# Feed-forward of a two-layer model: seven block products per matrix in place of eight

## The reference, cut to what matters

```python
x = x + merged @ w_out[l]
h2 = rmsnorm_2(x, g_mlp[l])
x = x + jnp.square(jax.nn.relu(h2 @ w_ff1[l])) @ w_ff2[l]        # w_ff1 1024x4096, w_ff2 4096x1024
ple_gate = jax.nn.sigmoid(rmsnorm_2(x, g_ple[l]) @ w_ple_gate[l])
x = x + (p[l] @ w_ple[l]) * ple_gate
return rmsnorm_2(x, g_final)
```

## Time and profile before

| | |
|---|---|
| median of 3 runs | 3937.43 us (3936.14 to 3940.52) |
| the profiled execution: its own time | 3931.09 us |
| the profiled execution: its span | 3929.4 us |
| mean granted TensorE clock | 0.959 |
| TensorE busy in the span | 3606.5 us (92%) |
| `Tail`, first matmul to end | 3021.8 to 3929.4 us |
| DMA in the feed-forward | 97 GB/s |

### The profile page before, as it was taken

The page is one execution under the profiler, slowest core; times in us unless marked ns, Lnnn a source line. Parts: engine busy times, 40 slices in busy tenths (PEclk is TensorE's granted clock), DMA queues, the critical chain, the costliest instruction groups (busy, mean ns, idle before and its releaser), DMA issues. The chain is left out here.

```text
span 3929.4 us, 44017 instructions
## 1 busy us (share of the span) xinstructions
PE 3606.5 (92%) x16732; PEld 2857.8 (73%) x16732; DVE 2196.8 (56%) x2464; ACT 1568.7 (40%) x2086; POOL 1111.4 (28%) x569
## 2 busy tenths in 40 slices
PE   7899998586999999779899999999798999999997
PEld 3678887465787878557677577777676888888886
DVE  5579467646888888767553322222255643353338
ACT  4322234535777777635223222222322332232233
POOL 1232210334111111234312122222243444444443
PEclk9899999797999999889999999999899999999999
DMA  5312346657999999834311311111354223333333
GB/s 196 97 54 88 121 141 205 208 179 272 399 395 402 402 396 402 346 137 153 134 65 60 109 59 62 66 57 58 129 182 140 96 92 97 98 96 97 97 113 123
DMA packets 176113, 650.33 MB, mean 166 GB/s; under 512 B 21392, under 2 KB 56560, under 8 KB 159824
## 3 DMA queue, kind: packets, MB, share of 16 engines
q1 hardware_dynamic: 134464, 553.24, 39.1%
q10 hardware_dynamic: 31696, 65.07, 4.4%
q0 software_dynamic: 9792, 29.81, 2.0%
HBM read 540.71 MB, written 107.34 MB: 165 GB/s over the span
## 5 line engine op out<-in xcount | busy, mean ns | idle before, releaser
L3743 POOL TENSOR_TENSOR t_wl<-t_raw,t_wh 128x1024 fp32r<-128x1024 f32 x160 | 386.8, 2418 | 521.1 <-ACT t_wh L3789 521.1
L100 PE MATMUL m_b<-b_high,m_high 128*128 128x512 f32 x960 | 404.6, 421 | 8.9 <-POOL m_low L2616 7.0
L102 PE MATMUL m_b<-b_high,m_low 128*128 128x512 f32 x960 | 382.8, 399 | 0.0
L101 PE MATMUL m_b<-b_rest,m_high 128*128 128x512 f32 x960 | 382.3, 398 | 0.0
L2614 POOL TENSOR_TENSOR m_high<-m_raw,m_one 128x1024 fp32r<-128x1024 f32 x60 | 119.0, 1983 | 796.9 <-PE m_b L102 727.7
L100 PE MATMUL t_b<-b_high,t_wh 128*128 128x512 f32 x768 | 301.9, 393 | 15.2 <-POOL t_wl L3743 15.2
L101 PE MATMUL t_b<-b_rest,t_wh 128*128 128x512 f32 x768 | 299.6, 390 | 0.0
L102 PE MATMUL t_b<-b_high,t_wl 128*128 128x512 f32 x768 | 299.6, 390 | 0.0
L3789 ACT ACTIVATE t_wh<-t_raw 128x1024 fp32r<-128x1024 f32 x160 | 169.1, 1057 | 311.4 <-PE t_b L102 290.4
L100 PE MATMUL zs_z<-zs_hs,zs_high 128*128 128x512 f32 (+1 forms) x584 | 226.8, 388 | 8.5 <-DVE zs_hs L310 8.0
L3882 DVE TENSOR_TENSOR t_x<-t_x,t_b 128x512 f32<-128x512 f32 x80 | 55.0, 687 | 317.2 <-PE t_b L102 317.2
(11 more groups left out here) (658 smaller groups left out, 8672.5 us busy)
## 6 DMA issues: line engine op xcount, KB each, us to landing
moe_raw<-in_expert_w SPq DMA_DIRECT2D x79, 2048.0 KB, 10.1
ex_raw<-in_expert_w SPq DMA_DIRECT2D x39, 2048.0 KB, 10.7
t_raw<-in_w_ff SPq DMA_DIRECT2D x128, 512.0 KB, 3.4
m_raw<-in_w_ug SPq DMA_DIRECT2D x60, 512.0 KB, 4.4
yrows<-ex_y ACTq DMA_DIRECT2D x38, 512.0 KB, 11.1
gates<-m_ob SPq DMA_DIRECT2D x32, 512.0 KB, 2.9
me_g<-gates SPq DMA_DIRECT2D x32, 512.0 KB, 3.7
zs_raw<-in_w_in_s SPq DMA_DIRECT2D x29, 512.0 KB, 3.5
```

Of the source, the lines that this page charges most:

```text
L100: nc.tensor.matmul(out, w[0], x[0], start=first, stop=False)
L101: nc.tensor.matmul(out, w[0], x[1], start=False, stop=False)
L102: return nc.tensor.matmul(out, w[1], x[0], start=False, stop=last)
L3743: self.nc.gpsimd.tensor_tensor(self.wl[u % self.NW][:], self.raw[u % 2][:], self.wh[u % self.NW][:].bitcast(F32), ALU.subtract).then_inc(s ...
```

## The change

Both matrix products are done by Strassen's scheme on 2x2 blocks: seven products of half the depth in each direction where the plain scheme has eight.

**First matrix.** w_ff1 is cut by input half (512 of 1024) and output half (tile g against tile g + 16), the tokens in two halves. For each of 16 pairs g there are 7 products of 4 x 3 = 12 matmuls (112 in all). Four of them need a sum of weight blocks (`weight_sum`, VectorE, 128x512), and four need a combination of blocks of the normalised x (made once, in place of x, `t_made`; x itself is first written to DRAM, `spill`). The seven PSUM results are combined by VectorE (`c11`, `u2`, `c12`, `c22`, `c21`) into four hidden tiles, which get relu and square in one VectorE instruction (`bend`), and five combinations of them (`mix`, `mix21`); seven tiles of 256 KB a pair are written to DRAM (`keep`).

**Second matrix.** Seven passes over 16 of those tiles each; a pass has 4 output groups of 4 chains' parts, 12 matmuls a part (112 parts, v = 0 to 111), one bank per group of 4 parts. Each part's weights are loaded as one or two 256 KB blocks (2 KB rows) and, in five of the seven passes, summed by VectorE (`weight_sum2`). The hidden tiles come back from DRAM one by one (`hidden`), each split again (`hid_high` ScalarE, `hid_low` VectorE). A group's bank is added to or subtracted from one or two tiles of x (`update`, 48 additions in all).

**Around them.** Weight tiles of WO and GATE keep 24 matmuls but share four wh/wl buffers of 128x512, so two units deep in place of three; raw is four tiles deep; seven banks in place of six. GATE units all come after the feed-forward. The hand-written order of the starts (`load`, `scalar`, `vector`) is new.

The diff, cut to its core; after the DMA queue (`load`) come a stretch of ScalarE with `evict(f)`, then VectorE from the start of the first matrix:

```diff
-    NB, NW, NHID, NPW = 6, 3, KD + 1, 8
+    NB, PAIRS, FIRST = 7, 16, 14
+    RING = (1, 2, 5, 6, 3, 7, 4)
+    PASSES = (((1, 0), (1, 1), 1, ((1, 0, 1), (1, 1, -1))),
+              ((1, 1), None, 0, ((0, 0, 1), (1, 0, 1))),
+              ((0, 0), (1, 1), 1, ((0, 0, 1), (1, 1, 1))),
+              ((0, 1), (1, 1), -1, ((0, 0, 1),)),
+              ((0, 0), (0, 1), 1, ((0, 0, -1), (0, 1, 1))),
+              ((0, 0), None, 0, ((0, 1, 1), (1, 1, 1))),
+              ((1, 0), (0, 0), -1, ((1, 1, 1),)))
+    def products(self):
+        return [(g, x) for x in (1, 2, 3, 5, 6, 7, 4) for g in range(2)] + [(g, x) for g in range(2, self.PAIRS) for x in self.RING]
...
+        def weights(v):
+            (r, c), second, _, _ = self.PASSES[v // 16]
+            n, q = v % 16 // 4, v % 4
+            if v >= 4:
+                sp.wait_ge(self.split, self.NF + v - 3)
...
+                sp.dma_start(self.raw[:, v % 4, half(i)], self.A["w_ff2"][n + 4 * r][:, a:a + BANK]).then_inc(self.ff2_in[v % 4], 16)
...
+        for g in range(self.PAIRS - 2):
+            sp.wait_ge(self.split, self.at[g, 4] + 1)
+            pair(g + 2)
+            keep_b11(g)
+            keep(g)
...
+        for v in range(8, self.NV):
+            weights(v)
+            if v + 12 < self.NV:
+                hidden(v + 12)
...
+        for f in range(10, self.NF):
+            evict(f)
+            high(f + 4)
+            for p in {105: range(0, 4), 106: range(4, 8), 107: range(8, 12), 108: range(12, 15), 110: range(15, 16)}.get(f, ()):
+                hid_high(p)
...
+        mean(1)
+        for x in (5, 6):
+            weight_sum(1, x)
+        invert(1)
+        for k in range(4, KD):
+            scale(1, k)
+            if k > 4:
+                y_low(1, k - 1, KD + k - 5)
+        weight_sum(1, 3)
+        y_low(1, KD - 1, KD + 3)
+        for j in range(4):
+            scale(1, j)
+        for j in range(4):
+            dve.wait_ge(self.scaled, KD + 4 + j + 1)
+            V.tensor_tensor(self.X(j, 0), self.X(j, 1), self.X(j, 0), ALU.subtract).then_inc(self.t_made, 1)
+        weight_sum(1, 7)
+        for j in range(4):
+            V.tensor_tensor(self.X(j, 1), self.X(4 + j, 1), self.X(j, 1), ALU.subtract).then_inc(self.t_made, 1)
+        t_low(0)
...
+        for g in range(2):
+            bend11(g)
+            bend12(g)
+            bend22(g)
+            mix(g)
+        weigh(18)
+        for g in range(2):
+            c21(g)
+            mix21(g)
...
+        def step(f):
+            g, x = self.order[f]
+            if x == 2:
+                c11(g)
+                bend11(g)
+            if x == 6:
+                u2(g)
+            if x == 3:
+                c12(g)
+                bend12(g)
+            if x == 7:
+                c22(g)
+                bend22(g)
+                mix(g)
+            if x == 4:
+                c21(g)
+                mix21(g)
+            weigh(f + 5)
...
+               hid=(7, 16, P, BANK))
...
+    A["w_ff1"], A["w_ff2"] = tiles(J["w_ff1"][0]), tiles(J["w_ff2"][0])
```

More of the change, by code:

```diff
@@ L3645 @@
 class Tail:
[L3651 to L3652 removed]
+    NB, PAIRS, FIRST = 7, 16, 14
+    RING = (1, 2, 5, 6, 3, 7, 4)
+    PASSES = (((1, 0), (1, 1), 1, ((1, 0, 1), (1, 1, -1))),
[6 rows of a table added]
+    NF, NV = 112, 112
+    WO_UNITS = GATES = 2 * KD
     def __init__(self, nc, s, A, R, C, out, high, rest, gains):
         self.nc, self.A, self.R, self.C, self.out, self.h, self.gains = nc, A, R, C, out, (high, rest), gains
[L3656 to L3662, removed]
[L3663 to L3676 removed]
@@ L3678, in order @@
[L3678 to L3714, removed]
+        self.order = self.products()
@@ new lines, in __init__ @@
+        self.at = {u: f for f, u in enumerate(self.order)}
+        first = [(g, x) for g in range(2) for x in (5, 6, 3, 7)]
+        sums = first + [u for u in self.order if u[0] >= 2 and u[1] in (5, 6, 3, 7)]
+        self.sum_at = {u: i + 1 for i, u in enumerate(sums)}
+        self.wsum_at, self.loads = [], []
+        for v in range(self.NV):
+            two = self.PASSES[v // 16][1] is not None
+            self.wsum_at.append((self.wsum_at[-1] if v else 0) + two)
+            self.loads.append((self.loads[v - 4] if v >= 4 else 0) + (32 if two else 16))
@@ L3718, in load, with spill @@
         tiles_of = lambda r, c: r.rearrange("k p t -> p k t")[:, :, half(c)]
[L3719 to L3723, removed]
+        def spill(i):
+            c, n = divmod(i, KD)
+            sp.wait_ge(self.added, i + 1)
+            sp.dma_start(self.R["xb"][n][:, half(c)], self.X(n, c)).then_inc(self.spilled[c], 16)
@@ new lines, in load @@
+        keep(14)
+        for p in range(4, 12):
+            hidden(p)
+        for v in range(2, 4):
+            weights(v)
+        keep_b11(15)
+        weights(4)
+        for p in range(12, 15):
+            hidden(p)
+        weights(5)
+        hidden(15)
+        weights(6)
+        for p in range(16, 20):
+            hidden(p)
+        weights(7)
+        keep(15)
+        for c in range(2):
+            sp.wait_ge(self.kept_b11[c], 128)
+            sp.wait_ge(self.kept[c], 96 * 8)
@@ new lines, in scalar @@
+        for u in range(2):
+            wo_high(u)
+        for u in range(self.WO_UNITS):
+            c, n = divmod(u, KD)
+            act.wait_ge(self.wo_used, u + 1)
+            if u + 2 < self.WO_UNITS:
+                wo_high(u + 2)
+            else:
+                for f in range(2):
+                    high(2 * (u + 2 - self.WO_UNITS) + f)
+            if u == KD:
+                root(0)
+            act.wait_ge(self.added, u + 1)
+            square(c, n)
+            if KD + 1 <= u < KD + 5:
+                for k in range(2 * (u - KD - 1), 2 * (u - KD)):
+                    y_high(0, k, k)
```

638 lines of the change are left out of this document (512 added, 126 removed).

## The result

The changed kernel takes **3914.88 us** (median of 4 runs, 3910.47 to 3918.32) against 3936.78 us for the kernel before in the same comparison (3932.81 to 3940.52): a ratio of 0.9945 with a 95% interval from 0.9931 to 0.9959, so 21.9 us faster (16 to 27). The forecast was 3882, that is 55 us; the sign held, the size did not. One run of before (4320 us, granted clock 0.80) and one of e4 (14617 us, 0.23) were slow, and the ratios leave them out.

The account below looks back on a forecast made before the run. TensorE's own work was taken to bound the kernel (busy 92% of the span). Removing 87.0 and 7.2 us and giving back 26, 6, 3, 1 and 3 made -55: 3882 us from 3937.4, range 3850 to 3930.

Parts of the forecast that it names:

- Removed: Feed-forward: 384 fewer matmuls at 0.2267 us save 87.0 us; the old hand-over's stall of 7.2 us goes too.
- First matrix, steady: 0: Steady pairs of the first matrix: VectorE and GpSimd keep up with TensorE's 19.04 us, adding 0, bounds 0 to 45.
- rival B: First matrix: VectorE sets the pace, 1.5 to 3.2 us a pair, adding 21 to 45: 3903 to 3927; chance 0.21.
- Second matrix, steady, and its loads: 0: Second matrix: VectorE and GpSimd keep pace (0, bounds 0 and 10), and 256 KB loads at 261 GB/s add 0.
- rival C: Second matrix: loads don't keep up, below 222 GB/s; at 200 GB/s the time is 3975 us; chance 0.08.
- Start of the first matrix: +26: First matrix's start: TensorE waits 19 us in early products and 7 more at product 19; bounds 12 and 40.
- Hand-over: +6, bounds 0 and 14: Passage from first to second matrix: VectorE's owed work, hidden-tile loads and x coming back cost 6 us.
- The term for VectorE's 33 instructions: Hand-over: 33 VectorE instructions and six GpSimd subtractions take 29 us before part 3, which TensorE reaches after 24.5.
- Gates: +3: Gates: two weight buffers and a sigmoid before each high part give six stalls, net 3 us, bounds 0 and 8.
- Norm: +3, WO: +1: Norm from part 92: late weight sums cost 3 us, bounds 0 and 8; WO's two buffers cost 1, bounds 0 and 3.
- Rivals D and E: D: starts and hand-over hidden, 3840 to 3850, chance 0.07. E: longer half-clock stretches, 3935 or so, chance 0.04.
- The prediction's own sign of being wrong: The forecast is wrong if the second matrix takes over 320 us or the first over 360.

Follow-up runs that it names:

- e4: Changed kernel with VectorE's instructions reordered at the start of the first matrix, low parts of x's combinations and last differences earlier: 3909.2 us.
- e1: Changed kernel with x loaded back one 0.5 MB tile at a time around parts 8 to 14, not 4 MB ahead of part 8: 3902.7 us.
- e9: Changed kernel with e1 to e4, x back more thinly, loads ahead of SyncE's wait for stored tiles, norm squares ahead of weight highs: 3882.6 us.
- e2: Changed kernel with hidden tiles 12 to 14 queued on SyncE ahead of the weights of parts 2 to 4: 3910.0 us.
- e11: e9 with GpSimd making only 8 of 512 columns of each feed-forward weight low part, the rest left out: 3860.6 us.
- e3: Changed kernel with three buffers for the gate weights in place of two: 3905.3 us.
- e5: Changed kernel with GpSimd making only 8 of 512 columns of each feed-forward weight low part, the rest left out: 3891.6 us.
- e12: e9 with all sixteen low parts of the combinations of x made by VectorE, where GpSimd made eight: 3883.2 us.

## Why the prediction came out as it did

**Removed.** Right. 384 matmuls fewer, 0.2267 us each: the steady stretches show it, and the tails agree.

**First matrix, steady: 0.** Right, and rival B is out: from product 21 to 110 nothing is added. The measured 3914.9 lies in B's 3903 to 3927, and that is luck: none of it comes from the steady pairs. (One sum there is off: 7 x 0.69 + 13 x 0.63 are 13.0 us, not 13.2, so a fully blocked pair would take 22.0.) The distinction made from the earlier trace rows held as well: in the steady stretch L4217, with SBUF inputs alone, has a mean of 1204 ns, L4209, with one in PSUM, 688.

**Second matrix, steady, and its loads: 0.** Right, and rival C is out. From part 16 to 91 nothing is added, and the changed kernel's parts with two blocks ran at 280 to 302 GB/s with no wait for a DMA. The Trainium skill (DMA: Bandwidth & Descriptors, Bandwidth) asks for 1 MiB a DMA; the streams of 256 KB here moved more than the 138 GB/s it gives for 64 KB, at a DMA share of 0.85 to 0.92. Its figures are for DMAs issued from GpSimd, and these are issued from SyncE.

**Start of the first matrix: +26.** Nearly right, 30.6 with 0.9 for the norm's sum: 3.7 more. Its own terms before product 14 are 1.2, 1.0, 12, 3 and 4, which make 21.2 and not 19, so with the 7 of product 19 it should have said 28, and the miss is then 1.5. Term by term the walk was further off than its sum (product 6 had 11.5 for 12, product 8 had 0.4 for 3, product 10 had 7.4 for 4, product 11 had 1.2, product 19 with 20 had 4.3 for 7). With short low parts and the order mended 12.6 is left, near the lower bound of 12 that I gave.

**Hand-over: +6, bounds 0 and 14.** This is the step that failed: 28.3 us (end 3.3, parts 1 to 4 11.0, parts 5 to 15 14.1), 22 of the 33 us by which the forecast missed, and outside the bounds. In it, "x comes back as 4 MB ahead of the weights of v = 8" was seen and even priced, 10 us at 410 GB/s, but with 4.5 of the +6 taken by VectorE's 33 instructions it can have counted for 1.5 at most, and the prediction gives no reason for the rest to be hidden. It was not: part 8 alone had 10.9. SyncE's queue is one line, and I counted its issues and not its waits: at that point it waits 3.7 us for the last tiles to be stored, so the lead is spent before the 4 MB start. e1 and e9 show this: 7.4 of the 13.5 us there go with the first, 2.7 more with the second, both by SyncE's order of issue (the other edit in e9 is at the start). The same for part 1: 2.5 was forecast, 6.4 and 6.9 measured, and 5.5 of it is gone with e2, which then bares the waits of parts 3 and 4.

The term for VectorE's 33 instructions, 4.5 at part 3, looks good beside the 4.1 that parts 3 and 4 have in e9, but that is luck. 7.7 of its 29 us are GpSimd's six subtractions; without them VectorE would be done in 21.5, ahead of TensorE's 24.5, and nothing would be left. In e11 they are 0.2 us each, and parts 3 and 4 still have 4.0. What the trace of e11 shows there is the last tile's way to DRAM and back, and half clock after that wait.

**Gates: +3.** Failed in size, 10.9 (9.4 in the second execution). The cause was named ("two buffers, a sigmoid before each high part"), but its six stalls make 7.5 us where the trace has some 15 (16.7 less two norm sums): they were added up gate by gate and come out at half. e3 shows that the third buffer alone is worth 7.8.

**Norm: +3, WO: +1.** 3.9 with the 0.9 of the sum, and 0.1: right. e5 takes the 3.0 of the norm away, by less blocking or by the earlier low part.

The sum of the misses: hand-over 22, gates 8, start 4, less 1 for WO, make 33. Rivals D and E fell: there are stalls of 10.75 us and half clock behind them, but only in short stretches. The prediction's own sign of being wrong came: the second matrix took 333.7 us, over 320.

What stays open: the cause of the 6 us that parts 1 to 4 keep in e9 and e11 was read from the traces and not tested by a run of its own; e9's 3.2 in parts 5 to 15; and how much of what the short low parts give is blocking.

## What to carry to other kernels

When a stage is shortened, walk each in-order queue through the seam, and the DMA queue first: every wait that it makes there (for stores, for a buffer) spends the lead of all loads behind it, and a large transfer then costs its full length. Put loads that can go ahead of such a wait, and split what must come back. Stalls by order and stalls by blocking hide each other, so an edit that looks worth 3 us alone may be worth 11 once the other is mended.

## What the runs showed that was not expected

GpSimd can be kept out for long. The Trainium skill (SBUF — State Buffer, SBUF: two separate sides) says that whichever of the two engines starts first holds the shared ports for its whole instruction and the other fully blocks; the traces agree, but it reads like turns of one instruction. In e12 GpSimd's 1.29 us subtraction took 10.11 while VectorE ran back to back with two SBUF inputs, and the four subtractions there took 18.60. In the changed kernel four scalings took 5.82 beside three subtractions, so there they did take turns. In e12 itself four scalings at 3134.42 also took 5.82. What decides between the two isn't settled here.

Leaving out most of GpSimd's low parts of the feed-forward weights is worth 23 us of tail (e9 against e11, 836.6 and 813.2), though VectorE is only 63% busy over the span of the changed kernel: 15 of it at the start, 3 to 4 each at the end of the first matrix and in the norm, 1 each in WO and in parts 5 to 15. That is an upper bound for what blocking costs there, since the low parts also come sooner. The gates have blocking too, which no run takes away.
